# Sixty-four weighted expert rows of a two-layer diffusion step: summed by GpSimd behind ScalarE, in place of VectorE

## The reference, cut to what matters

```python
def trunk_layer(x, cond, lp, rope, ctx):
    ...
    x = x + g1 * mix
    hff = rmsnorm(x, lp['norm2_g']) * (1 + sc2) + sh2
    x = x + g2 * peer_ffn(hff, lp['peer_wq'], lp['peer_keys'], lp['peer_u'], lp['peer_v'])

def peer_ffn(h, w_q, sub_keys, u_tab, v_tab):     # per block of 128 tokens hb
        q = (hb @ w_q).reshape(PEER_BLOCK, PEER_HEADS, 2, PEER_QDIM // 2)
        ...                                       # idx, best_s: 16 experts for each of 8 heads
        gate = jax.nn.softmax(best_s, axis=-1).astype(hb.dtype)
        act = jax.nn.gelu(jnp.einsum('thkd,td->thk', u_tab[idx], hb), approximate=False)
        return jnp.einsum('thk,thkd->td', gate * act, v_tab[idx])
```

## Time and profile before

| | |
|---|---|
| median of 3 runs | 4766.85 us (4754.92 to 4771.77) |
| the profiled execution | 4754.92 us, span 4753.1 us |
| busy: PE / DVE / POOL / ACT | 78% / 69% / 31% / 16% |
| DMA queue of the gathers | 70.4% of 16 engines' span |
| DVE L1349, the rows added by DVE | 62 at about 1.28 us |
| PE L984, query projection | 288.9 us in all |

### The profile page before, as it was taken

The page is one execution under the profiler, slowest core; times in us unless marked ns, Lnnn a source line. Parts: engine busy times, 40 slices in busy tenths (PEclk is TensorE's granted clock), DMA queues, the critical chain, the costliest instruction groups (busy, mean ns, idle before and its releaser), DMA issues.

```text
span 4753.1 us, 36060 instructions
## 1 busy us (share of the span) xinstructions
PE 3722.7 (78%) x10798; PEld 1832.8 (39%) x10798; DVE 3297.5 (69%) x8263; ACT 760.8 (16%) x2269; POOL 1458.1 (31%) x1284
## 2 busy tenths in 40 slices
PE   7578687888787778788878686788977778777776
PEld 6463444643232223235535443355422323222222
DVE  1636885676888868754574768656688787786665
ACT  0121135221101010010121112441110100101001
POOL 0001131213444535432222012222144444444332
PEclk9789898999999999999989898898999999999999
DMA  8244465766999999999979354657599999999998
GB/s 273 90 130 166 172 222 206 270 248 267 418 418 408 421 418 415 421 379 391 373 257 359 116 194 176 225 206 283 195 398 421 410 421 421 411 421 421 403 421 336
DMA packets 342147, 1497.69 MB, mean 315 GB/s; under 512 B 31424, under 2 KB 176448, under 8 KB 178112
## 3 DMA queue, kind: packets, MB, share of 16 engines
q0 software_dynamic: 184320, 1342.26, 70.4%
q1 hardware_dynamic: 157632, 153.13, 10.0%
HBM read 1491.97 MB, written 3.31 MB: 315 GB/s over the span
## 4 chain that ended last, share of the span: by engine, by line
PE 35%; DMA 31%; DVE 25%; issue 4%; ACT 4%; SPq 1%; POOL 0%; DVEq 0%; ACTq 0%; POOLq 0%
DMA uv_ring<-uv,expert_index 24%; PE expert_acc L747 13%; DVE uv_ring L1328 6%; PE rotating L984 6%; DMA arena<-uv,expert_index 5%; PE rotating L956 3%; PE rotating L776 3%; DVE diag L1337 2%; PE rotating L810 2%; DVE arena L1328 2%; DVE arena L1497 2%; DVE arena L1710 1%; DMA w_ring<-w_ada 1%; PE rotating L727 1%; PE rotating L815 1%
## 5 line engine op out<-in xcount | busy, mean ns | idle before, releaser
L747 PE MATMUL expert_acc<-uv_ring,diag 128*128 128x512 f32 x3504 | 1758.2, 633 | 455.7 <-DVE diag L1337 447.8
L701 POOL DMA_INDIRECT uv_ring<-uv,expert_index x940 | 1067.3, 1135 | 2801.3 <-PE expert_acc L747 2117.6
L747 PEld LDWEIGHTS expert_acc<-uv_ring,diag 128*128 128x128 f32 x3504 | 635.4, 196 | 1442.8 <-DVE diag L1337 915.7
L1328 DVE CUSTOM_DVE_ANT_0 uv_ring<-uv_ring,arena 128x1024 f32<-128x1024 f32 x684 | 836.3, 1223 | 237.8 <-DMA uv_ring<-uv,expert_index 235.9
L747 PE MATMUL expert_acc<-arena,diag 128*128 128x512 f32 x1360 | 678.3, 625 | 176.1 <-DVE diag L1337 145.1
L1042 ACT ACTIVATE gelu<-u_dot 128x1 f32<-128x1 f32 x1280 | 258.9, 203 | 2821.0 <-DVE u_dot L1328 2820.3
L1337 DVE TENSOR_SCALAR diag<-const_mats,expert_gate,gelu 128x128 f32<-128x128 f32 x1216 | 442.0, 363 | 273.7 <-ACT gelu L1042 186.4
L701 POOL DMA_INDIRECT arena<-uv,expert_index x340 | 390.5, 1149 | 450.0 <-PE expert_acc L747 434.1
L1328 DVE CUSTOM_DVE_ANT_0 arena<-arena 128x1024 f32<-128x1024 f32 x340 | 415.9, 1223 | 94.1 <-DMA arena<-uv,expert_index 92.1
L747 PEld LDWEIGHTS expert_acc<-arena,diag 128*128 128x128 f32 x1360 | 239.2, 193 | 596.0 <-DVE diag L1337 374.7
L1328 DVE CUSTOM_DVE_ANT_0 uv_ring<-uv_ring,prompt_rows 128x1024 f32<-128x1024 f32 x256 | 312.3, 1220 | 60.0 <-DMA uv_ring<-uv,expert_index 59.5
(11 more groups left out here) (207 smaller groups left out, 2851.5 us busy)
## 6 DMA issues: line engine op xcount, KB each, us to landing
w_ring<-w_ada SPq DMA_DIRECT2D x66, 512.0 KB, 12.3
w_ring<-w_in SPq DMA_DIRECT2D x64, 512.0 KB, 5.0
w_ring<-w_pq SPq DMA_DIRECT2D x64, 512.0 KB, 6.8
w_ring<-w_out SPq DMA_DIRECT2D x32, 512.0 KB, 7.6
uv_ring<-w_ada SPq DMA_DIRECT2D x30, 512.0 KB, 5.6
uv_ring<-uv,expert_index POOLq DMA_INDIRECT x940, 11.5
arena<-b_ada SPq DMA_DIRECT2D x48, 128.0 KB, 5.9
arena<-uv,expert_index POOLq DMA_INDIRECT x340, 15.9
```

Source lines behind the costliest of these rows:

```text
L701: pool.indirect_dma_start(out=UV[j], out_offset=None, in_=uv, in_offset=bass.IndirectOffsetOnAxis(ap=idxs[:, n % 2, k:k + 1], axis=0)).the ...
L747: ins = pe.matmul(acc[:, half, :], diag[:, TURN[m] % DIAGS, :], UV[SLOT_AT[m]][:, D + 512 * half:D + 512 * half + 512], start=(k == 0), st ...
L1328: V_.tensor_tensor_reduce(UV[j][:, 0:D], UV[j][:, 0:D], rows_of(n), 1.0, 0.0, ALU.mult, ALU.add, dots[:, m % DOTS:m % DOTS + 1]).then_inc( ...
```

## The change

The same 64 slots are summed by POOL in place of DVE. ACT, which computed the weight, now also scales v by it, in place in the ring's buffer (a second activation of 128x1024 behind each weight, with a wait for the weight between). POOL clears the sum once a layer and then adds each scaled row with a tensor_tensor. DVE's `add_row` goes. The slot numbers, the steps of `Beside`, the fold and everything else stay.

```diff
+            def add_row(m, first):
+                n = m // SLOTS
+                if first:
+                    if n % NBLK == 0:
+                        pool.wait_ge(*s_sup.at(n // NBLK, 1, 7))
+                    else:
+                        pool.wait_ge(s_pup.sem, n)
+                    nc.gpsimd.memset(pool_sum(n), 0.0).then_inc(pool_chain, 1)
+                    pool.wait_ge(pool_chain, FOLDS.index(n) + 1)
+                else:
+                    pool.wait_ge(s_pa, TURN[m])
+                pool.wait_ge(s_pw, TURN[m] + 1)
+                nc.gpsimd.tensor_tensor(pool_sum(n), UV[SLOT_AT[m]][:, D:2 * D], pool_sum(n), ALU.add).then_inc(s_pa, 1)
...
+                            while added < len(mine) and mine[added] <= SLOT_BEFORE[m]:
+                                add_row(mine[added], added == 0)
+                                added += 1
                             if k == 0:
                                 pool.wait_ge(*s_idx.at(l, g, 2 * b))
...
                             pool.indirect_dma_start(out=UV[j], out_offset=None, in_=uv,
                                                     in_offset=bass.IndirectOffsetOnAxis(ap=idxs[:, n % 2, k:k + 1], axis=0)).then_inc(s_gat[j], 16)
+                        for i in range(added, len(mine)):
+                            add_row(mine[i], i == 0)
...
                 act.wait_ge(s_gel, m + 1)
-                nc.scalar.activation(weight[:, m % DOTS:m % DOTS + 1], gel[:, m % DOTS:m % DOTS + 1], ACT.Copy,
-                                     scale=gat[:, n % 2, k:k + 1]).then_inc(s_wt, 1)
+                chain(nc.scalar.activation(weight[:, m % DOTS:m % DOTS + 1], gel[:, m % DOTS:m % DOTS + 1], ACT.Copy,
+                                           scale=gat[:, n % 2, k:k + 1]))
+                v = UV[SLOT_AT[m]][:, D:2 * D]
+                nc.scalar.activation(v, v, ACT.Copy, scale=weight[:, m % DOTS:m % DOTS + 1]).then_inc(s_pw, 1)
...
-            def add_row(n, k):
-
-                m = n * SLOTS + k
-                v, w = UV[SLOT_AT[m]][:, D:2 * D], weight[:, m % DOTS:m % DOTS + 1]
-                dve.wait_ge(s_wt, TURN[m] + 1)
-                if not any(by_dve(n, i) for i in range(k)):
-                    ins = V_.tensor_scalar(dve_sum(n), v, w, None, ALU.mult)
-                else:
-                    dve.wait_ge(s_va, TURN[m])
-                    ins = V_.scalar_tensor_tensor(dve_sum(n), v, w, dve_sum(n), ALU.mult, ALU.add)
-                ins.then_inc(s_va, 1)
-
...
-                if 1 <= m <= SLOTS:
-                    (add_row if by_dve(n, m - 1) else weigh)(n, m - 1)
+                if 1 <= m <= SLOTS and not by_pool(n, m - 1):
+                    weigh(n, m - 1)
```

More of the change, by code:

```diff
@@ L191, with by_pool @@
 SLOT_AT, SLOT_BEFORE, SLOT_TURN = slot_buffers()
-DVE_FROM, DVE_ALL = 84, 108
-def by_dve(n, k):
-    return n % NBLK == 0 and (k >= DVE_FROM and k % 2 == 1 or k >= DVE_ALL)
+POOL_FROM, POOL_ALL = 84, 108
+def by_pool(n, k):
+    return n % NBLK == 0 and (k >= POOL_FROM and k % 2 == 1 or k >= POOL_ALL)
 def sums_before(n, k):
-    slots = [by_dve(m // SLOTS, m % SLOTS) for m in range(n * SLOTS + k)]
+    slots = [by_pool(m // SLOTS, m % SLOTS) for m in range(n * SLOTS + k)]
     return slots.count(False), slots.count(True)
[L210 to L213, removed]
+PE_SLOTS = [m for m in range(L * NBLK * SLOTS) if not by_pool(m // SLOTS, m % SLOTS)]
+POOL_SLOTS = [m for m in range(L * NBLK * SLOTS) if by_pool(m // SLOTS, m % SLOTS)]
+TURN = {m: i for of in (PE_SLOTS, POOL_SLOTS) for i, m in enumerate(of)}
+FOLD_AFTER = {n: SLOTS + 2 for n in range(L * NBLK) if any(by_pool(n, k) for k in range(SLOTS))}
 FOLDS = sorted(FOLD_AFTER)
@@ L475, in build, with pool_sum @@
         psum_out = at(ARENA - 512, 512)
-        def dve_sum(n):
+        def pool_sum(n):
             return htok[1] if n % NBLK == 0 else htok_p[:]
@@ L531, in build @@
         s_dg = ctx.enter_context(nc.semaphore("diag_ready"))
-        s_wt = ctx.enter_context(nc.semaphore("expert_weight_ready"))
-        s_va = ctx.enter_context(nc.semaphore("v_added_by_vector"))
-        s_fold = ctx.enter_context(nc.semaphore("vector_sum_folded"))
+        s_pw = ctx.enter_context(nc.semaphore("v_weighted"))
+        s_pa = ctx.enter_context(nc.semaphore("v_added_by_pool"))
+        s_fold = ctx.enter_context(nc.semaphore("pool_sum_folded"))
         s_vs = ctx.enter_context(nc.semaphore("v_summed"))
@@ L537, in build @@
         act_chain = ctx.enter_context(nc.semaphore("act_chain"))
+        pool_chain = ctx.enter_context(nc.semaphore("pool_chain"))
         class Chain:
@@ L557, in summed @@
         def summed(eng, m):
-            if by_dve(m // SLOTS, m % SLOTS):
-                eng.wait_ge(s_va, TURN[m] + 1)
+            if by_pool(m // SLOTS, m % SLOTS):
+                eng.wait_ge(s_pa, TURN[m] + 1)
             else:
@@ L564, in all_summed @@
         def all_summed(eng, n):
-            pe_slots, dve_slots = sums_before(n, 0)
+            pe_slots, pool_slots = sums_before(n, 0)
             eng.wait_ge(s_vs, pe_slots)
-            if dve_slots:
-                eng.wait_ge(s_va, dve_slots)
+            if pool_slots:
+                eng.wait_ge(s_pa, pool_slots)
         def w_unit(l, g, kind, u):
@@ L689, in _ @@
                         n = blk(l, g, b)
+                        mine = [n * SLOTS + k for k in range(SLOTS) if by_pool(n, k)]
+                        added = 0
                         for k in range(SLOTS):
@@ L751, in fold @@
             def fold(n):
-                pe.wait_ge(s_va, sums_before(n + 1, 0)[1])
+                pe.wait_ge(s_pa, sums_before(n + 1, 0)[1])
                 for half in range(2):
-                    ins = pe.matmul(acc[:, half, :], C[:, C_ID, :], dve_sum(n)[:, 512 * half:512 * half + 512],
+                    ins = pe.matmul(acc[:, half, :], C[:, C_ID, :], pool_sum(n)[:, 512 * half:512 * half + 512],
                                     start=False, stop=(FOLD_AFTER[n] > SLOTS), skip_group_check=True)
@@ L759, in add_beside @@
             def add_beside(n, m):
-                if 2 <= m <= SLOTS + 1 and not by_dve(n, m - 2):
+                if 2 <= m <= SLOTS + 1 and not by_pool(n, m - 2):
                     add_v(n, m - 2)
@@ L1053, in gelu_beside @@
                     gelu(n, m)
-                    if by_dve(n, m):
+                    if by_pool(n, m):
                         weigh(n, m)
```

## The result

The changed kernel takes 4830.6 us in the median of its runs (4806.97 to 4834.71), the kernel before 4769.3 us in the same comparison: ratio 1.0117, interval 1.0097 to 1.0139, so 46 to 66 us slower, 56 by the ratio (the two medians stand 61 apart). 4805 us were forecast, with a range of 4776 to 4842. The profiled execution has a span of 4819.6 us.

The account below looks back on a forecast made before the run. PE set the pace before; POOL was to become the bound in query tiles 0 to 7. Fold +16.4 us (norm's 1.2 included) plus 2.6 made 19.0 a layer, twice 38: 4793 us, 4805 set on the median; range 4776 to 4842.

Parts of the forecast that it names:

- Output projection, taken at 0: Output projection, steps 84 to 107: PE's waits for DVE stay as they are, 0 gain and loss.
- My bound of five times 2.3: Output projection: at most, a POOL add in DVE's way at each of five places where PE waits, 11 us.
- rival (b): Query tiles: POOL and DVE exclude each other, stretching gathers or holding up dots; 4824 or 4840 us; chance 0.24.
- Second norm, +1.2 us: Second norm: ACT's new scaling stands between slot 107's weight and the first square, +1.2 us a layer.
- A slot at 4.06 us: Query tiles: POOL's time per slot, gaps 0.6, gather issue 1.17 and add 2.29 us, against PE's 3.6.
- Start and end: Query tiles: gather for slot 113 goes out at 994.9 us; gather for 127 at 1051.7, fold at 1064.5.
- Behind the stall, 2.6 us: After PE's idle time of about 17 us, the following tiles run partly at a lower clock: 2.6 us a layer.
- the forecast's own case: Query tiles: POOL becomes the bound at 3.6 to 4.4 us a slot, fold 16.4 us later; chance 0.50.
- its mildest form: Query tiles: dots coming during POOL's adds start afterwards and stretch the next gather; 4.7 us a slot, 4824 us.
- Rival (a): Query tiles: POOL's add costs only 1.22 us, POOL is no bound, fold +2.8 us a layer, 4772 us; chance 0.14.
- Rival (c): Query tiles: POOL's add costs up to 4.6 us, 6.4 us a slot, 4874 us; chance 0.08.
- Rival (d): Output projection and fold: DVE, rid of 32 rows a layer, comes earlier for PE; at best 4753 us; chance 0.04.

Follow-up runs that it names:

- write-only kernels: Two kernels: the changed kernel with each GpSimd add replaced by clearings of the sum, two (4783.5 us, ratio 1.0048) or three (4796.1 us, ratio 1.0053).
- 2.4 us clearings: The changed kernel with each GpSimd add replaced by three clearings, 2.45 us in all, 64 rows left out of the result: 4796.1 us, ratio 1.0053.

## Why the prediction was right or wrong

The direction, the place and the mechanism were right: PE waits at the fold, for POOL, in both layers, and the total lies in the range. The size was short, 38 us against 56 by the ratio (46 to 66). By its own steps, layer 1:

- *Output projection, taken at 0.* Wrong: 4.0 us (92.76 to 96.78). I looked only at the five places where PE waited already, and there its waits stayed as forecast. The loss came at three others, behind tiles 4, 8 and 12, where PE had a little slack: POOL's add began 0.2 us ahead of the diag, which took 2.38 us, and PE now waits 0.45 us for it. That is 1.5 us more idle time in the stage; the other 2.5 are longer matmuls, of which the clock level can be 1.7. My bound of five times 2.3 named the mechanism, not the places; rival (b) had it in the query tiles only, and I gave the sum no share of it here. The run with GpSimd at this place alone shows the diags and the waits.
- *Second norm, +1.2 us.* 1.0 measured, in every run in which ACT scales.
- *A slot at 4.06 us.* 4.12, but by luck: two errors cancel. I took gaps of 0.6, and they are 0.3 (almost none between a gather and the add behind it). I took the gather at 1.17, and it averaged 1.42 over the fourteen, since ten of the fifteen gathers of the stage were stretched by a dot, nine of them to 1.65; the add averaged 2.40.
- *Start and end.* The gather for slot 113 went out 7.5 us behind the hT writes, not 5.7. A dot held up the add ahead of it by 0.3 us; the other 1.5 are a gap of 1.78 us between that add and the gather, where 0.27 us follow the later adds. The write-only kernels have the same gap, layer 2 has none, and the kernel before already idled 2.18 us ahead of this gather in layer 1, so it is not rival (b); its cause is open. From the gather for 127 to the fold 15.0 us passed, not 12.8: the last two dots took 3.35. With the 2.4 us clearings it was 13.4, so 1.5 of these 2.2 us are rival (b).
- *Behind the stall, 2.6 us.* The fold and the steps to tile 8 took 7.1 us in place of 4.5, tiles 0 to 7 0.8 less than before.

So the forecast's own case (POOL as the bound) is 12 to 15 us of a layer's 27, and rival (b) 8 to 14: 6 to 10 at the fold and 2.3 to 4 at the output projection. I had given (b) 0.24. That its mildest form was priced at 4824 us, close to what was measured, is luck: it had a slot at 4.7 us, which took 4.12, and nothing at the output projection or at the end. The Trainium skill (SBUF — State Buffer, "SBUF: two separate sides") has an operation with two on-chip inputs and a reading one of GpSimd exclude each other for a whole instruction, and an operation in a two-port mode any of GpSimd's. The runs agree: dots of 3.35 us beside adds, 1.22 beside clearings, diags of 2.38 beside adds, and diags of 0.80 beside clearings, which end with the clearing as the others end with the add.

Rival (a), a cheap add, fell with 2.37 us, and its price was too low. It had POOL no bound at 3.0 us a slot, since PE asks for one every 3.6, and a loss of 5.6 us. With half an add, 3.07 us a slot, POOL still ended last, and the loss was 15 us (9 to 21), of which the two layers' stages show 8.7. The comparison of 4.06 with 3.6 in my own case has the same fault; the sum does not, since it added up start, slots and end. Rival (c) fell. Rival (d), that DVE's relief would help PE, fell: DVE's rows are not late for PE. The runs with *more* of them gain, because each takes 1.8 us of work from PE at the output projection, and the diags that PE waited for go with it.

Open: 12 us by which the profiled executions differ beyond the two layers' 54 (66 in all). 6.8 of them lie ahead of slot 84 in layer 1, where nothing was changed, and 6.6 between the two layers' stages. The profiled execution before was a quick one, 14 us under its median, and without any new work on GpSimd (ScalarE's scaling alone) the stretch between the layers was 12.7 us longer than in it. So these 12 us may be spread between executions; that is not shown. And the ratio of the 2.4 us write-only run is 6 us lower than its stages' 32 us; this was not followed up.

## What to carry to other kernels

An engine that issues the gathers is not free when it is 31% busy: its work goes ahead of each gather, in order, and its time per slot (here 0.3 + 2.4 + 1.4 us) is paid at each of them. Do not compare it with the pace of the fed engine alone (3.6 us): add the start ahead of the first gather, all slots, and what lies behind the last gather, and set that against the whole stretch of the engine that waits. Here 3.07 us a slot were still too much. Ask of each operation moved to GpSimd which VectorE operations will run beside it: here they, too, wait for each other. Look also at places where nothing waits yet, since a small slack can be used up. Where PE is the bound, look for products to give away before giving away the rows of an engine that has time.

## What the runs showed of the hardware

- A GpSimd float32 add of 128x1024 takes 2.34 to 2.37 us undisturbed, 128x512 1.27, a clearing of 128x1024 0.95 to 0.97. DVE's add of the same shape takes 1.22.
- A dot that meets such an add, and a gather's issue that meets a dot, are prolonged by about what is left of the other (1.22 to up to 4.0 us; 0.95 to 1.65). Beginning first does not always save it: three dots (at 1024.23, 1057.32 and 3408.82 us in the changed kernel) began during a gather's issue, 0.15 to 0.6 us ahead of the add, and took 3.6 to 4.0 us.
- A diag of 0.34 us that meets an add or a clearing ends 0.1 us behind it, having taken 2.38 to 2.41 or 0.80 us. A dot beside a clearing stays at 1.22.
- Between a GpSimd add or clearing and a gather's issue that waits for its semaphore 0.27 us pass; between two adds in a row, the second of which waits for the first, 0.08.
